# A two-layer transformer tail: where one projection stands around the first scores, and where the first heads' output product stands

## What is computed

```python
for layer in range(DEPTH_2):                     # 2
    h = rmsnorm(x, norm_mix[layer])
    z = h @ w_in[layer]
    ...                                          # split z into q, k, v, gates of four mixers
    o_a = nsa_mixer(...)                         # units "cmp", "slc", "win"
    o_b = diff_mixer(...)                        # units "diff"
    o_c = mlstm_mixer(...)                       # units "mlstm"
    o_d = dilated_mixer(...)                     # units "dil"
    x = x + jnp.concatenate([o_a, o_b, o_c, o_d], axis=-1) @ w_out[layer]
    h = rmsnorm(x, norm_ffn[layer])
    x = x + (jax.nn.silu(h @ w_gate[layer]) * (h @ w_up[layer])) @ w_down[layer]
return rmsnorm(x, norm_final)
```

## Time and profile before

| | |
|---|---|
| median of 3 runs | 2002.72 us (1999.62 to 2007.18) |
| the profiled execution's own time | 1994.0 us |
| its span in the trace | 1992.1 us |
| TensorE busy | 1677.0 us, 84% of the span |
| VectorE, ScalarE busy | 700.0 us (35%), 356.0 us (18%) |
| granted clock of TensorE, mean | 0.912 |
| first `mixing` stage, last product of outputs | from 1157 us to 1349.8 us |
| second `mixing` stage | the same 413.2 us later |

### The profile page before, as it was taken

How to read it: one execution, slowest core, us unless ns; L and a number is a source line. 1 busy time by engine, 2 the same in 40 slices (tenths; PEclk the granted TensorE clock), 3 DMA queues, 4 the chain that set the end, 5 groups by cost and what they waited for, 6 DMA issues and landing times.

```text
span 1992.1 us, 31970 instructions
## 1 busy us (share of the span) xinstructions
PE 1677.0 (84%) x14184; PEld 1141.1 (57%) x14184; DVE 700.0 (35%) x1247; ACT 356.0 (18%) x827; POOL 91.0 (5%) x94
## 2 busy tenths in 40 slices
PE   6999899987989676645655689998999899899997
PEld 2665458957975432211211257758994476669963
DVE  2006372463332300000000024564665244646663
ACT  2010212342231220000000022421010124310000
POOL 0000003402311000000000000000000000000000
PEclk8999898987999788778778889999999999999999
DMA  9431111040014599999999963213545532225440
GB/s 393 185 117 53 68 45 43 4 170 2 4 63 174 211 382 427 428 428 428 427 427 428 428 222 120 85 43 148 190 175 206 188 120 85 85 85 209 168 184 21
DMA packets 35593, 382.08 MB, mean 192 GB/s; under 512 B 6977, under 2 KB 10433, under 8 KB 12673
## 3 DMA queue, kind: packets, MB, share of 16 engines
q1 hardware_dynamic: 35458, 380.04, 47.6%
HBM read 378.98 MB, written 1.05 MB: 191 GB/s over the span
## 4 chain that ended last, share of the span: by engine, by line
PE 50%; DMA 11%; DVE 3%; ACT 1%; issue 1%; SPq 0%; DVEq 0%; ACTq 0%
PE psum L2761 14%; PE psum L1873 7%; PE psum L2832 7%; DMA arena<-in_w_moe 7%; PE psum L2168 6%; DMA weight_ring<-in_w_moe 5%; PE psum L2171 3%; PE psum L1848 3%; PE psum L2319 3%; PE psum L2309 1%; PE psum L1828 1%; PE psum L2288 1%; PE psum L2274 1%; PE psum L2197 1%; PE psum L2251 0%
## 5 line engine op out<-in xcount | busy, mean ns | idle before, releaser
L1873 PE MATMUL psum<-weight_ring,arena 128*32 128x512 f32 x640 | 142.0, 719 | 128.3 <-DMA arena<-in_w_moe 94.1
L1269 PE MATMUL psum<-arena 64*64 64x64 f32 x4608 | 150.8, 223 | 19.6 <-PEq L962 8.8
L2761 PE MATMUL psum<-arena 128*128 128x128 f32 x1408 | 165.2, 275 | 1.7 <-DVE arena L2965 1.7
L2761 PEld LDWEIGHTS psum<-arena 128*128 128x128 f32 x1408 | 161.1, 192 | 2.0 <-issue 2.0
L1269 PEld LDWEIGHTS psum<-arena 64*64 64x64 f32 x4608 | 143.2, 138 | 27.0 <-issue 22.8
L1873 PEld LDWEIGHTS psum<-weight_ring,arena 128*32 128x32 f32 x640 | 36.0, 129 | 205.5 <-issue 205.5
L2002 DVE COPY arena<-psum 128x512 f32<-128x512 f32 x16 | 11.1, 692 | 371.3 <-PE psum L1873 371.3
L1873 PE MATMUL psum<-arena 128*32 128x512 f32 x384 | 106.5, 715 | 33.6 <-DMA weight_ring<-in_w_moe 33.1
L2761 PE MATMUL psum<-arena,weight_ring 128*128 128x128 f32 x1056 | 129.8, 280 | 4.7 <-ACT arena L2879 2.6
L2761 PEld LDWEIGHTS psum<-arena,weight_ring 128*128 128x128 f32 x1056 | 125.2, 196 | 6.0 <-DVE arena L2969 2.8
L2168 PE MATMUL psum<-arena,weight_ring 128*128 128x256 f32 x512 | 123.6, 394 | 0.0
(11 more groups left out here) (497 smaller groups left out, 2226.2 us busy)
## 6 DMA issues: line engine op xcount, KB each, us to landing
weight_ring<-in_w_moe SPq DMA_DIRECT2D x60, 2048.0 KB, 20.2
arena<-in_w_moe SPq DMA_DIRECT2D x36, 2048.0 KB, 20.5
weight_ring<-in_w_in SPq DMA_DIRECT2D x23, 2048.0 KB, 8.7
weight_ring<-in_w_mod SPq DMA_DIRECT2D x12, 2048.0 KB, 8.0
weight_ring<-in_w_gate SPq DMA_DIRECT2D x12, 2048.0 KB, 7.6
weight_ring<-in_w_up SPq DMA_DIRECT2D x12, 2048.0 KB, 7.5
weight_ring<-in_w_down SPq DMA_DIRECT2D x12, 2048.0 KB, 7.6
weight_ring<-in_w_out SPq DMA_DIRECT2D x6, 2048.0 KB, 7.6
```

What stands on the lines that cost most here:

```text
L1269: last = nc.tensor.matmul(K.ps[half[d], bank, column + HD * n:column + HD * n + HD], lhs(d, h), rhs(d, h), start=True, stop=True, skip_gro ...
L1873: last = nc.tensor.matmul(K.ps[strip(j), 4, :], xsT[:, k, CAP * e:CAP * e + CAP], ws[j][:, k, :], start=(k == 0), stop=(k == KT - 1), skip ...
L2761: last = nc.tensor.matmul(K.ps[:, bank, P * n:P * n + P], lhs, rhs, start=(n == 0 and k == 0 and name in ("m1", "m5", "m6")), stop=(k == 3 ...
```

## The change

Six places of two functions are edited. On TensorE, `j7` is cut in two around `score(0)`; at unit 5 the first half of `j16` goes ahead of `score(6)`; at unit 9 `values(9)` goes ahead of `qk0`. At the end the product of tile 1 moves from banks 2 and 3 to banks 0 and 1, and the turned outputs `o3`, `o1`, `o2` from banks 0 and 1 to 2 and 3. With that `out_product(0, 1)` is cut up: two of its matmuls before `values(13)`, one before `o3`, one behind it; and `out_product(3, 1)` goes ahead of `o1`. In `feed_forward`, `m1` of unit 1 goes ahead of `m1` of unit 0, and the wait for x stands between them.

```diff
-    late = {"o3": 0, "o1": 1, "o2": 0}
+    late = {"o3": 2, "o1": 3, "o2": 2}
...
-        out_bank = lambda t, n: 6 + n if t == 0 else 2 + n
+        out_bank = lambda t, n: 6 + n if t == 0 else n
...
+        half_job(first_fill, 0)
         score(0)
-        item(first_fill)
+        half_job(first_fill, 1)
         for u in range(NU):
+            if u == 5:
+                half_job(halved[u], 0)
             if u + 1 < NU:
                 score(u + 1)
             if u in leads:
                 item(leads[u])
-            if u in halved:
+            if u in halved and u != 5:
                 half_job(halved[u], 0)
             turn(u)
             if u in halved:
                 half_job(halved[u], 1)
             for name in fills[u]:
+                if name == "qk0":
+                    values(u)
                 item(name)
...
-            values(u)
-        pe.wait_ge(scores_kept, NU)
-        pe.wait_ge(pt_kept, NU)
+            if u == NU - 1:
+                pe.wait_ge(scores_kept, NU)
+                out_product(0, 1, (0, 1))
+            if "qk0" not in fills[u]:
+                values(u)
+        out_product(0, 1, (2,))
         item("o3")
-        out_product(0, 1)
+        out_product(0, 1, (3,))
         out_product(3, 0)
+        out_product(3, 1)
         item("o1")
         item("o2")
-        out_product(3, 1)
...
-            product(0, "m1", ws[0], 0)
-            pe.wait_ge(x_in, x_at[1])
             product(1, "m1", ws[1], 3)
+            pe.wait_ge(x_in, x_at[1])
+            product(0, "m1", ws[0], 0)
```

More of the change, by code:

```diff
@@ L2312, in tensor, with out_product @@
         ws = []
-        out_bank = lambda t, n: 6 + n if t == 0 else 2 + n
-        def out_product(g, t):
+        out_bank = lambda t, n: 6 + n if t == 0 else n
+        def out_product(g, t, parts=range(4)):
             kept(f"o{g}")
[L2317 to L2322, removed]
+            for part in parts:
+                k, n = 2 * g + part // 2, part % 2
+                last = nc.tensor.matmul(K.ps[:, out_bank(t, n), :], K.mixT[:, k, P * t:P * t + P], ws[n][:, k, :],
+                                        start=(g == 0 and k == 0), stop=(g == 2 and k == 5))
+                if g == 0 and t == 0 and part == 0:
+                    last.then_inc(W.used, 1)
             if g == 2:
@@ L2688, in vector @@
             dve.wait_ge(out_made, t + 1)
-            nc.vector.tensor_tensor(K.x[:, t, :], K.x[:, t, :], K.ps[:, 6 - 4 * t:8 - 4 * t, :].rearrange("p a b -> p (a b)"),
+            nc.vector.tensor_tensor(K.x[:, t, :], K.x[:, t, :], K.ps[:, 6 - 6 * t:8 - 6 * t, :].rearrange("p a b -> p (a b)"),
                                     ALU.add).then_inc(x_ready, 1)
@@ L2717, in feed_forward @@
     names = ("m1", "m6", "m5", "m7", "m2", "m4", "m3")
-    early = [("m1", 0), ("m1", 1), ("m2", 0), ("m2", 1)]
+    early = [("m1", 1), ("m1", 0), ("m2", 0), ("m2", 1)]
     steps = early + [(n, u) for u in range(2 * FCH) for n in names if (n, u) not in early]
@@ L2780, in first_units @@
             pe.wait_ge(t_kept, 1)
+            product(1, "m1", ws[1], 3)
+            pe.wait_ge(x_in, x_at[1])
             product(0, "m1", ws[0], 0)
-            pe.wait_ge(x_in, x_at[1])
-            product(1, "m1", ws[1], 3)
             turn_input(1)
```

## The result

The changed kernel took 1983.71 us (median of 4 runs, 1980.38 to 1988.32) against 2001.74 us of the kernel before (4 runs, 1999.62 to 2007.18): a ratio of 0.9907, interval 0.9879 to 0.9936, so 18 us faster. I had forecast 10.7 us and 1992.0 us with a range that began at 1986.0.

What follows compares the result with a forecast made beforehand. TensorE's idle time and lower clock inside the two `mixing` stages were taken to bound the kernel. Gains of 14.1 us less 3.4 at the tail gave 10.7, so 2002.7 - 10.7 = 1992.0 us, range 1986 to 1999.5.

Steps and rivals of the forecast that it cites:

- The first scores: Half of `j7` ahead of `score(0)` fills TensorE's 2.11 us wait and keeps the clock up: 3.56 us gained a layer.
- Unit 5: Half of `j16` ahead of `score(6)` fills the 1.24 us wait, clock held: 2.56 us gained a layer.
- Unit 9: `values(9)` ahead of `qk0` covers its 0.85 us of idle time: 0.95 us gained a layer.
- The tail: End of the units: TensorE idles 3.6 us for the `o3` copy, plus clock cost; 2.4 us lost layer 0, 1.0 layer 1.
- The feed-forward edit: `m1` of unit 1 ahead of unit 0's delays a copy that eight transposes hide: zero.
- The sum: Gains of 14.1 us in both layers less 3.4 us at the tail: 10.7 us faster.
- T2: Theory in the experiments: the change is worth 18 us, and the profiled execution of before happened to be cheap.
- (a): Rival: the clock falls at the old places in the units all the same; about 1998 us, chance 0.16.
- (b): Rival: units hang on VectorE and ScalarE, the 0.6 us slack at `turn(0)` turns negative; about 1999 us, chance 0.08.
- (e): Rival: the 3.6 us idle at the tail drops the clock through the output products; slower, 2011 us, chance 0.04.
- (c): Rival: the tail costs two half-clock stretches each time, 3.6 us more; about 1995.6 us, chance 0.10.
- (d): Rival: the tail costs no clock, 3.2 us less; about 1989 us, chance 0.08.

Runs made afterwards that it cites:

- first two profiles: Profiled executions of the kernel before and the changed kernel, no edit: spans 1992.1 and 1982.2 us.
- third profile of the change: Changed kernel a third time, no edit, against the kernel before: its profiled execution spans 1990.5 us, stages 146.5 us each.
- second and third comparison: Changed kernel again, no edit, twice against the kernel before: 1987.03 us, ratio 0.9943, then 1987.36 us, ratio 0.9951.
- 2006.79 us execution: Kernel before with ScalarE's copy of `o3` moved ahead of the square root: one execution, 2006.79 us, stages 150.90 and 152.45 us.
- second of the change: Profile of the changed kernel timed again, no edit, beside the kernel before: median 1987.03 us, ratio 0.9943, stages 146.5 us each.

## Why the prediction was wrong in the level and right in the steps

**The first scores (3.56 us a layer).** Right, and 0.2 us too high: 3.35 and 3.4 us by themselves. From `score(0)` to `score(1)` it is 2.57 us where the working had 2.38, because the second half of `j7` takes 1.9 us to the next issue and not 1.74. The clock held wherever the wait was filled to 0.38 us, in all 14 cases of seven traced executions.

**Unit 5 (2.56 us).** Right: 2.6 us in layer 0 by itself. The limits that the prediction named are in the rows: ScalarE's logarithm ahead of `keep(5)`, and the copy of `j16` ahead of `j17`, with 0.16 us of waiting.

**Unit 9 (0.95 us).** Right, 0.9 to 1.0 us. The three together gave 6.95 us a layer, 7.07 forecast.

**The tail (2.4 us lost in layer 0, 1.0 in layer 1).** Right: the change gains 4.5 and 6.0 us where its units gain 6.95 in each layer, so 2.5 and 1.0 us were lost against the kernel before; by itself the tail cost 2.5 in layer 0. (Against the units alone it is 2.45 us in both layers, since there the old tail had the shorter low stretch in layer 1 too.) The wait was 3.79 us (3.6 forecast), its cause is the place of the copy on ScalarE, and the clock cost behind it 1.9 us (1.6 taken). The sentence that nothing helps it since the copy "does not depend on where TensorE has got to" holds only for that order on ScalarE.

**The feed-forward edit (nothing).** Right, 0.02 us.

**The sum.** 10.7 us forecast; 10.4 between the stages of the first two profiles, 11.0 from `score(0)` to the end of the launch (11.2 in the third profile of the change), 11.5 and 10.0 by the medians of the second and third comparison (1998.5 - 1987.03 and 1997.37 - 1987.36).

**What failed is the last step**, "Its median runs lie 8.7 us above it, at 2002.72, so I predict 2002.7 - 10.7". I took the median of three runs as the level of the program, and passed over the profiled execution at 1994.0, which lay 5.6 us below the lowest of the three. In 42 later executions the kernel before lay between 1993.55 and 2002.92, with medians of 1996.84, 1998.5 and 1997.37. From 1997.4 the same 10.7 us lead to 1986.7, and the changed kernel's medians were 1983.7, 1987.0 and 1987.4. Of the 8.3 us by which 1992.0 missed, 5.3 are this level. The other 3.0 are 0.3 of the steps, and for the rest that the first four executions of the change lay below its later ones; why they did is open. The range was too narrow for the same reason: it took in what the steps could do and one sentence of "a run's noise", where the first block alone moved the start of `score(0)` from 1195.6 to 1211.7 us between executions.

That the sum of the steps came so close owes a little to luck: 1.6 us of the 11.0 is the low stretch near 1551 us, which eight of the 14 profiles have and the four of the change have not, and behind the second stage 1.1 us is lost. The prediction had neither.

T2 is out: neither the stages nor the two later ratios (0.9943 and 0.9951, both intervals reach down to no less than 0.9927) bear 18 us. That the four executions of before in the first comparison had a long first block is what fits, as the 2006.79 us execution above shows it can happen; none of the four has a trace, so it is argued and not shown. Nor is it excluded that a part of their level belonged to the chip: the later comparisons ran on four chips, and on which the first ran is not known. The stage lengths do not depend on it: the change has its 146.5 us on three of the four. Of the rivals of the prediction, (a), (b) and (e) are refuted by the rows; (c) and (d) did not happen in any of the traced executions of the change, where one stretch of 3.4 us followed the wait each time, in eight cases of four profiles (the old feed-forward order among them).

## What to carry to other kernels

Work moved ahead of a wait pays twice while the wait also brings the lower clock, but look at what the moved work was covering elsewhere: here three quarters of a product were taken out of the shadow of a copy, and that cost 2.45 us a layer of the 7 gained. When an engine waits for a small copy, look first at what stands ahead of the copy on its own engine; one line moved on ScalarE brought more than any single move on TensorE. And a level comes from many executions: when the profiled one lies outside the timed ones, the forecast has two levels to choose from, and its range must hold both.

## What the hardware showed that I had not expected

The same wait does not always bring the same clock. Behind the unfilled 2.11 us at the first scores the granted clock fell to 1.2 GHz in 10 of 12 cases, behind the 1.24 us at unit 5 in 13 of 14, and behind 1.24 us left at the first scores in 0 of 2; behind 0.38 us in 0 of 14. Nor does the length alone decide: a wait of 1.18 us for a copy of ScalarE (`qk1`, 1303.63 us in the kernel before) stands in both layers of all 14 profiles, and behind it the clock never fell. The Trainium skill (TensorE: Matmul & The Clock Gate, Part 1) has the gate run free of the program, and the waits that brought the lower clock only in some cases agree. They are the exceptions, though: at the old tail the three profiles with the timing of before all have 3.4 us of the lower clock in layer 0 and 6.8 in layer 1. The Trainium skill, in the same part, also has the lower clock come only after at least one idle window, where the rows have it after 1.24 us.

The start of the launch is one place where executions part. By 42 us six of the 14 profiles are about 5 us behind the others, in the same code, and none makes it up later. The run of sixteen small matmul records at 25 us tells the two kinds apart: 2.0 to 2.3 us long in eight profiles, 3.6 in the six. Here it is in the first profile of before, the second of the change and the third of the change, with the window of each behind it:

```profile
25.33 1.95 PE L248 MATMUL psum<-arena 128*128 128x2 f32 x16
25.49 3.57 PE L248 MATMUL psum<-arena 128*128 128x2 f32 x16
25.71 3.58 PE L248 MATMUL psum<-arena 128*128 128x2 f32 x16
```

```profile
25.00:35.00 10.00, 9.09 (x70) 5.78 (x66) 6.07 (x14) 3.50 (x7) 0.00 (x0) 1.00 1.00 424
25.00:35.00 10.00, 10.00 (x53) 9.18 (x50) 4.03 (x7) 2.58 (x5) 0.00 (x0) 0.58 1.00 426
25.00:35.00 10.00, 10.00 (x50) 9.29 (x47) 3.40 (x5) 2.25 (x4) 0.00 (x0) 1.00 1.00 424
```

The granted clock does not settle the cause. It reads 0.57 to 0.59 in three of the six and 1.00 in the other three, though the matmuls take as long. Further steps of 3 to 4 us, of either sign, come between 200 and 630 us in six of the profiles; their cause was not looked for.
